# Splitting the 512-column matmul of a compensated projection into 256-column matmuls that alternate between the halves of a PSUM bank

## The chip, the cores and the metric

The kernel runs on one core of a Trainium2 chip. The metric is the device time of one execution in microseconds (us): the median of three runs before the change is 1472.32 us (1472.12 to 1472.53). A number in ns is marked so.

## The reference

The kernel computes one layer of a hybrid decoder trunk on a sequence of 256 tokens with 2048 features, in float32. What matters here are its projections:

```python
h = rms_norm(x, norm_mix_g[l])
proj = h @ w_in[l]                      # 2048 x 10240
...                                      # HGRN2, S5 and stick-breaking mixers on proj, a GLU (512 x 1024)
merged = sum_k sigmoid(gate_k) * (branch_k @ w_branch[k])   # 3 x (512 x 2048), shortened
x = x + merged @ w_out[l]               # 2048 x 2048
hf2 = rms_norm(x, norm_ffn_g[l])
up = causal_depthwise_conv(hf2 @ w_up[l], conv_w[l])        # 2048 x 11264
x = x + (jax.nn.silu(up[..., :D_FF]) * up[..., D_FF:]) @ w_down[l]   # 5632 x 2048
```

## The kernel before

**Tiles and blocks.** Everything is transposed: a tile of a projection is 128 output features (partitions) by 256 tokens (columns), and it is a sum over blocks. A block is one 128x128 piece of a weight matrix times 128 input features by 256 tokens. The projections that go through the function `piece` have 3680 blocks: 80 tiles of 16 blocks for w_in (1280), 8 tiles of 4 for the GLU (32), 16 tiles of 16 for w_out (256), 88 tiles of 16 for w_up (1408) and 16 tiles of 44 for w_down (704).

**Three passes.** To keep float32 accuracy with the type fp32r, each weight and each input is split in a high and a low part, and a block is three products: high weight times high input, high weight times low input, low weight times high input. Inputs lie in SBUF as `[P, k, 2, SEQ]`, the high part's 256 columns ahead of the low part's 256. So one matmul of 512 columns (L295) with the high weight writes the whole PSUM bank: columns 0 to 255 hold the sum with the high input, 256 to 511 that with the low input. A second matmul of 256 columns (L297) adds the low weight's product to columns 0 to 255. When a tile is complete, ScalarE copies the upper half of the bank to SBUF (`copy_half`, L577) and VectorE adds the lower half to it (`add_halves`, L846). There are four such banks, used in turn.

**The branches** go through another function, `branch_piece` (L309): its three passes are three matmuls of 256 columns, all into columns 0 to 255 of the bank; 192 blocks in all.

**The ring of weights.** Weights come in pieces of up to 8 blocks (512 KB). The DMA queue of SyncE loads a piece into one of four `raw` buffers (L245), ScalarE rounds it to `w_hi` (L570), VectorE subtracts to get `w_lo` (L841), TensorE multiplies and increments `piece_used`. ScalarE waits for `piece_used` before it overwrites a `w_hi`, VectorE waits for ScalarE, TensorE waits for `lo_ready`, and SyncE waits for `lo_ready` before it reloads a `raw`.

**Order of the work.** Every engine has its program written out by hand. During the w_in projection (tiles n = 0 to 79) the work of the three mixers is woven in between tiles: the tables AT and TABLE_AT (L95 to L101) say after which tile each engine does which part. TensorE's mixer products are plain float32 matmuls (`fp32_product`, L328), VectorE's and GpSimd's mixer steps stand in the same in-order programs as the weights' `w_lo`. Behind w_in come the GLU, the branches, w_out, w_up and w_down, in loops.

Of the kernel before, what the change touches and what calls it, by code (L numbers as in the profile page):

```python
# [45 lines left out]
P = 128  # L46
D_MODEL = 2048
SEQ = 256
# [66 lines left out]
def layer(nc, xT, w_in, w_glu, w_br, w_out, w_up, w_down, norm_mix, norm_ffn, hg_gain, s5_small, s5_b, s5_c,  # L115
          s5_skip, sb_gain, conv, out):
    ctx = ExitStack()
    with ctx:
# [75 lines left out]
        bank = [ctx.enter_context(nc.psum_tensor(f"bank{b}", [P, 512], F32)) for b in range(BANKS)]  # L194
# [92 lines left out]
        def _(pe):  # L287
            def piece(b, p, c, blocks, rhs, first, last):

                if p is not None:  # L290
                    pe.wait_ge(lo_ready, p + 1)
                w, l = w_hi[c % RING], w_lo[c % RING]
                for n, k in enumerate(blocks):
                    a = rhs(n)
                    pe.matmul(bank[b][:, :], w[:, k * P:(k + 1) * P], a.rearrange("p a t -> p (a t)"),  # L295
                              start=first and n == 0, stop=False, skip_group_check=True)
                    mm = pe.matmul(bank[b][:, 0:SEQ], l[:, k * P:(k + 1) * P], a[:, 0, :],  # L297
                                   start=False, stop=last and n == len(blocks) - 1, skip_group_check=True)
                return mm

            def branch_piece(b, p, c, lo, src):
# [145 lines left out]
            def a_in_block(n, k):  # L447
                if n == 0:
                    pe.wait_ge(S("a_in_lo"), k + 1)
                return a_in[:, k, :, :]  # L450

            for n in range(IN_TILES):
                bank_free(n)
                for h in range(2):
                    mm = piece(n % BANKS, 2 * n + h, 2 * n + h, range(PIECE), lambda k: a_in_block(n, PIECE * h + k), h == 0, h == 1)
                    mm.then_inc(piece_used, 1)
                mixers(n)
# [3 lines left out]
            for m in range(CT):  # L461
                for i in range(2):
                    n = GLU_T + 2 * m + i
                    bank_free(n)
                    mm = piece(n % BANKS, GLU_P + m if i == 0 else None, GLU_P + m, range(CT * i, CT * (i + 1)),
                               lambda k: glu_in[:, k, :, :], True, True)
                    mm.then_inc(piece_used if i else S("glu_first"), 1)
# [19 lines left out]
            def after(sem, j, k, src):  # L487

                if j == 0:
                    pe.wait_ge(S(sem), k + 1)  # L490
                return src[:, k, :, :]

            with pe.Fori(0, OUT_TILES // BANKS) as i:
                for j in range(BANKS):
                    bank_free(i * BANKS + (OUT_T + j))
                    for h in range(2):
                        mm = piece(j, i * (2 * BANKS) + (OUT_P + 2 * j + h), 2 * j + h, range(PIECE),
                                   lambda k: after("merged_lo", j, PIECE * h + k, a_in), h == 0, h == 1)
                        mm.then_inc(piece_used, 1)
# [17 lines left out]
            with pe.Fori(0, DOWN_TILES // BANKS) as i:  # L517
                c = 0
                for j in range(BANKS):
                    bank_free(i * BANKS + (DOWN_T + j))  # L520
                    at = 0
                    for blocks in DOWN_PIECES:
                        if j == 0:
                            pe.wait_ge(S("act_lo"), at + blocks)
                        mm = piece(j, i * (BANKS * len(DOWN_PIECES)) + (DOWN_P + c), c, range(blocks),
                                   lambda k: act[:, at + k, :, :], at == 0, at + blocks == FT)
# [947 lines left out]
```

## Time and profile before

| what | value |
|---|---|
| median of 3 runs | 1472.32 us |
| the profiled execution's own time | 1471.41 us |
| its span (first to last instruction) | 1469.7 us |
| TensorE busy with matmuls | 1414.2 us, 96% of the span |
| VectorE busy | 1079.3 us, 73% |
| ScalarE busy | 761.9 us, 52% |
| GpSimd busy | 380.2 us, 26% |
| mean granted TensorE clock | 0.988 of 2.4 GHz |

Times are those of one execution under the profiler. PE is TensorE's matmul side, PEld its weight loads (which run beside matmuls), DVE is VectorE, ACT is ScalarE, POOL is GpSimd. The duration that a matmul's row shows goes from its start to its last result, and consecutive matmuls overlap; the distance between two starts is what a matmul takes in a stream.

### The profile page before, as it was taken

What the parts mean: (1) busy time and instruction counts of PE and PEld (TensorE: products, weight loads), DVE (VectorE), ACT (ScalarE), POOL (GpSimd) and SP (SyncE); (2) the same over time, 40 slices, a digit from 0 to 9 for tenths busy, and PEclk for the clock granted to TensorE, in tenths of its full rate; (3) what the DMA queues carried; (4) which work ended last, traced back from release to release, by engine and by line L of the source; (5) the groups of instructions that cost most, each with busy time, mean ns of one, the idle gap of its engine ahead of it and who ended that gap; (6) DMA issues with size and microseconds to landing.
All of it is one profiled execution on the core that took longest, in us unless ns stands there. A gap on an engine that the chain in (4) does not pass through costs nothing.

```text
span 1469.7 us, 24906 instructions
## 1 busy us (share of the span) xinstructions
PE 1414.2 (96%) x8320; PEld 1248.5 (85%) x8320; DVE 1079.3 (73%) x1370; ACT 761.9 (52%) x1050; POOL 380.2 (26%) x337
## 2 busy tenths in 40 slices
PE   5999999998888989999999999999999999999999
PEld 4889888887666878998888888888888888888887
DVE  5897757879999957777668777777777776544543
ACT  5564456675344445444565555555555554444432
POOL 5044312254966631332211111111111110000000
PEclk9999999999998999999999999999999999999999
DMA  7555544453434455565556555656555555666663
GB/s 216 175 175 170 166 151 161 150 182 108 144 128 151 151 165 195 200 214 186 187 173 205 194 183 188 197 181 194 191 181 197 187 186 187 182 213 202 189 202 111
DMA packets 74338, 261.45 MB, mean 178 GB/s; under 512 B 8560, under 2 KB 9104, under 8 KB 74160
## 3 DMA queue, kind: packets, MB, share of 16 engines
q1 hardware_dynamic: 73152, 256.41, 54.0%
q0 software_dynamic: 992, 4.37, 0.8%
q8 instruction: 31, 0.51, 0.1%
q14 instruction: 19, 0.16, 0.0%
q10 hardware_dynamic: 144, 0.01, 0.0%
HBM read 258.66 MB, written 2.10 MB: 177 GB/s over the span
## 4 chain that ended last, share of the span: by engine, by line
PE 76%; DVE 14%; issue 4%; POOL 2%; ACT 2%; DMA 1%; SPq 0%; POOLq 0%; ACTq 0%; DVEq 0%
PE bank L295 48%; PE bank L297 25%; DVE w_lo L841 5%; DVE tmp L849 3%; PE pair L328 2%; DVE tmp L1092 2%; DVE tmp L856 1%; DMA gates<-xT 1%; PE bank L309 1%; ACT w_hi L570 1%; POOL proj L1280 1%; POOL merged L1371 1%; POOL merged L1373 1%; DVE gates L846 0%; DVE proj L846 0%
## 5 line engine op out<-in xcount | busy, mean ns | idle before, releaser
L841 DVE TENSOR_TENSOR w_lo<-raw,w_hi 128x1024 fp32r<-128x1024 f32 x500 | 632.1, 1274 | 321.0 <-ACT w_hi L570 317.2
L570 ACT ACTIVATE w_hi<-raw 128x1024 fp32r<-128x1024 f32 x500 | 512.1, 1030 | 438.7 <-PE bank L297 380.1
L295 PE MATMUL bank<-a_in,w_hi 128*128 128x512 f32 x1536 | 553.9, 401 | 42.7 <-DVE w_lo L841 40.8
L295 PE MATMUL bank<-h,w_hi 128*128 128x512 f32 x1408 | 488.4, 390 | 0.0
L297 PE MATMUL bank<-a_in,w_lo 128*128 128x256 f32 x1536 | 438.8, 286 | 0.0
L297 PE MATMUL bank<-h,w_lo 128*128 128x256 f32 x1408 | 397.1, 282 | 0.0
L295 PEld LDWEIGHTS bank<-a_in,w_hi 128*128 128x128 f32 x1536 | 295.2, 192 | 114.6 <-issue 35.5
L295 PEld LDWEIGHTS bank<-h,w_hi 128*128 128x128 f32 x1408 | 264.2, 188 | 55.4
L297 PEld LDWEIGHTS bank<-a_in,w_lo 128*128 128x128 f32 x1536 | 297.2, 194 | 0.5 <-issue 0.5
L297 PEld LDWEIGHTS bank<-h,w_lo 128*128 128x128 f32 x1408 | 266.1, 189 | 0.0
L295 PE MATMUL bank<-act,w_hi 128*128 128x512 f32 x704 | 244.1, 390 | 0.0
L297 PE MATMUL bank<-act,w_lo 128*128 128x256 f32 x704 | 198.5, 282 | 0.0
L1398 POOL TENSOR_TENSOR padded<-sum_u,rstd 128x256 f32<-128x256 f32 x88 | 73.8, 839 | 413.2 <-DVE sum_u L846 400.4
L295 PEld LDWEIGHTS bank<-act,w_hi 128*128 128x128 f32 x704 | 132.1, 188 | 27.7
L297 PEld LDWEIGHTS bank<-act,w_lo 128*128 128x128 f32 x704 | 133.1, 189 | 0.0
L1311 POOL TENSOR_TENSOR gates<-gates,rstd 128x256 f32<-128x256 f32 x48 | 57.8, 1210 | 155.9 <-DVE gates L846 155.1
L577 ACT ACTIVATE half<-bank 128x256 f32<-128x256 f32 x208 | 75.6, 366 | 9.0 <-PE bank L297 9.0
L1311 POOL TENSOR_TENSOR proj<-proj,rstd 128x256 f32<-128x256 f32 x32 | 32.9, 1038 | 135.6 <-DVE proj L846 99.1
L782 ACT ACTIVATE silu<-convd 128x256 f32<-128x256 f32 x43 | 18.0, 418 | 96.0 <-DVE convd L1214 96.0
L1212 DVE SCALAR_TENSOR_TENSOR convd<-padded,taps,convd 128x256 f32<-128x256 f32 x88 | 62.8, 713 | 1.0 <-ACT convd L802 1.0
L1214 DVE SCALAR_TENSOR_TENSOR convd<-padded,taps,convd 128x256 f32<-128x256 f32 x88 | 53.9, 613 | 11.5
L1280 POOL TENSOR_TENSOR proj<-tmp 128x512 f32<-128x512 f32 x32 | 56.3, 1760 | 1.9
(165 smaller groups left out, 1083.3 us busy)
## 6 DMA issues: line engine op xcount, KB each, us to landing
raw<-w_up SPq DMA_DIRECT2D x176, 512.0 KB, 3.3
raw<-w_in SPq DMA_DIRECT2D x160, 512.0 KB, 4.0
raw<-w_down SPq DMA_DIRECT2D x80, 512.0 KB, 4.3
raw<-w_out SPq DMA_DIRECT2D x32, 512.0 KB, 3.8
raw<-w_br SPq DMA_DIRECT2D x16, 512.0 KB, 3.6
raw<-w_br SPq DMA_DIRECT2D x16, 256.0 KB, 3.4
raw<-w_down SPq DMA_DIRECT2D x16, 256.0 KB, 2.7
gates<-xT SPq DMA_DIRECT2D x4, 512.0 KB, 10.4
```

Of the source, the lines that this page charges most:

```text
L295: pe.matmul(bank[b][:, :], w[:, k * P:(k + 1) * P], a.rearrange("p a t -> p (a t)"), start=first and n == 0, stop=False, skip_group_check= ...
L297: mm = pe.matmul(bank[b][:, 0:SEQ], l[:, k * P:(k + 1) * P], a[:, 0, :], start=False, stop=last and n == len(blocks) - 1, skip_group_check ...
L328: mm = pe.matmul(out_[p0:p1, c0:c1], lhsT, rhs, start=start, stop=stop, skip_group_check=True)
L570: act_e.activation(w_hi[s][:, 0:blocks * P], raw[s][:, 0:blocks * P], ACT.Copy).then_inc(hi_ready, 1)
L577: act_e.activation(half[j % 2][:, :], bank[j % BANKS][:, SEQ:2 * SEQ], ACT.Copy).then_inc(half_copied, 1)
L841: ve.tensor_tensor(w_lo[s][:, w], raw[s][:, w], w_hi[s][:, w].bitcast(F32), ALU.subtract).then_inc(lo_ready, 1)
L849: link(ve, ve.tensor_tensor(out_, a, b, op), name)
L1212: ve.scalar_tensor_tensor(c, padded[:, j % 2, 1:SEQ + 1], taps[:, t, 1:2], c, ALU.mult, ALU.add).then_inc(S("tap1"), 1)
L1214: ve.scalar_tensor_tensor(c, padded[:, j % 2, 0:SEQ], taps[:, t, 0:1], c, ALU.mult, ALU.add).then_inc(S("conv_done"), 1)
L1280: link(pool, pool.tensor_tensor(out_, a, b, op), name)
L1311: pool.tensor_tensor(proj(n), proj(n), rstd[:, :], ALU.mult).then_inc(tile_scaled, 1)
L1398: pool.tensor_tensor(padded[:, j, 2:], sum_u[:, j, :], rstd[:, :], ALU.mult).then_inc(S("up_scaled"), 1)
```

## The change

In `piece`, the 512-column matmul and the 256-column matmul of a block become three matmuls of 256 columns. For an even block of a piece they go to the lower, upper and lower half of the bank: high weight with high input, high weight with low input, low weight with high input. For an odd block the first two are exchanged, and the halves are upper, lower, upper: high weight with low input, high weight with high input, low weight with high input. So consecutive matmuls never write the same half. What a half holds differs from before, the sum of the two halves doesn't. Only the first matmul of a tile has the start flag. `branch_piece`, the mixers' products and all other engines stay as they are.

```diff
                 for n, k in enumerate(blocks):
                     a = rhs(n)
-                    pe.matmul(bank[b][:, :], w[:, k * P:(k + 1) * P], a.rearrange("p a t -> p (a t)"),
-                              start=first and n == 0, stop=False, skip_group_check=True)
-                    mm = pe.matmul(bank[b][:, 0:SEQ], l[:, k * P:(k + 1) * P], a[:, 0, :],
-                                   start=False, stop=last and n == len(blocks) - 1, skip_group_check=True)
+                    cols = slice(k * P, (k + 1) * P)
+                    passes = ((w, 0), (w, 1), (l, 0)) if n % 2 == 0 else ((w, 1), (w, 0), (l, 0))
+                    for m, (x, part) in enumerate(passes):
+                        at = (n + m) % 2 * SEQ
+                        mm = pe.matmul(bank[b][:, at:at + SEQ], x[:, cols], a[:, part, :], start=first and n == 0 and m == 0,
+                                       stop=last and n == len(blocks) - 1 and m == 2, skip_group_check=True)
                 return mm
```

## Rows read from the trace of the kernel before

**Rows 1.** Busy time by stretch of the span, in us (x instructions).
```profile
core 0: us, PE busy (x) PEld busy (x) DVE busy (x) ACT busy (x) POOL busy (x), PEclk, DMA share, GB/s
57.00:340.00 283.00, 281.29 (x1670) 248.30 (x1670) 221.72 (x246) 168.75 (x199) 95.44 (x68) 1.00 0.50 164
340.00:524.00 184.00, 153.21 (x858) 126.89 (x858) 169.34 (x167) 79.30 (x92) 131.03 (x79) 0.93 0.44 143
649.00:1470.00 821.00, 816.42 (x4708) 723.52 (x4708) 560.86 (x737) 418.61 (x618) 96.79 (x123) 1.00 0.58 187
```

**Rows 2.** Waits of TensorE from 340 to 524 us: total, times, longest.
```profile
PE bank L295 <- DVE w_lo L841: 24.6, 10, 4.9
PE pair L328 <- POOL proj L1280: 6.2, 2, 4.4
```

**Rows 3.** Waits of TensorE from 524 us to the end.
```profile
PE bank L309 <- DVE o_s L1136: 1.5, 1, 1.5
PE bank L295 <- DVE a_in L1151: 0.8, 1, 0.8
```

**Rows 4.** Other engines' waits, 340 to 524 us.
```profile
ACT w_hi L570 <- PE bank L297: 63.3, 32, 5.9
DVE w_lo L841 <- ACT w_hi L570: 8.5, 10, 1.5
DVE proj L1097 <- PE pair L328: 2.8, 1, 2.8
```

**Rows 5.** Line L295: duration ns min/median/max, first and last start in us.
```profile
L295 PE MATMUL bank<-h,w_hi x1408: 390/390/588, 733.3 to 1221.5; 128*128 128x512 f32 x176
L295 PE MATMUL bank<-act,w_hi x704: 390/390/390, 1221.9 to 1465.6; 128*128 128x512 f32 x176
```

**Rows 6.** TensorE in order of time, w_up: start us, us.
```profile
899.80 0.39 PE L295 MATMUL bank<-h,w_hi 128*128 128x512 f32 x1
900.03 0.28 PE L297 MATMUL bank<-h,w_lo 128*128 128x256 f32 x1
900.15 0.39 PE L295 MATMUL bank<-h,w_hi 128*128 128x512 f32 x1
```

**Rows 7.** Line L309 from 580 to 643.65 us, columns as in rows 5.
```profile
L309 PE MATMUL bank<-o_hg,w_hi x120: 277/279/281, 580.5 to 640.5; 128*128 128x256 f32 x120
```

**Rows 8.** TensorE in order of time, branches: a block's first two matmuls a row.
```profile
587.53 0.39 PE L309 MATMUL bank<-o_s,w_hi 128*128 128x256 f32 x2
...
587.88 0.40 PE L309 MATMUL bank<-o_s,w_hi 128*128 128x256 f32 x2
...
588.58 0.40 PE L309 MATMUL bank<-o_s,w_hi 128*128 128x256 f32 x2
...
588.93 0.39 PE L309 MATMUL bank<-o_hg,w_hi 128*128 128x256 f32 x2
...
589.28 0.40 PE L309 MATMUL bank<-o_hg,w_hi 128*128 128x256 f32 x2
```

**Rows 9.** TensorE in order of time: plain float32 products of a mixer.
```profile
288.11 0.59 PE L328 MATMUL pair<-tmp,lower 128*128 128x256 f32 x2
288.54 0.38 PE L328 MATMUL pair<-tmp,ones 128*128 128x128 f32 x2
288.76 0.60 PE L328 MATMUL pair<-tmp,lower 128*128 128x256 f32 x2
```

**Rows 10.** TensorE in order of time, at a granted clock of 0.5.
```profile
33.08 0.63 PE L295 MATMUL bank<-a_in,w_hi 128*128 128x512 f32 x1
33.51 0.41 PE L297 MATMUL bank<-a_in,w_lo 128*128 128x256 f32 x1
33.72 0.63 PE L295 MATMUL bank<-a_in,w_hi 128*128 128x512 f32 x1
```

**Rows 11.** Weight loads by line, form and tile: count, busy us, mean ns.
```profile
L297 PEld LDWEIGHTS bank<-a_in,w_lo 128*128 128x128 f32 x1536 | 297.2, 194 | 0.5 <-issue 0.5
L309 PEld LDWEIGHTS bank<-o_hg,w_hi 128*128 128x128 f32 x128 | 19.5, 188 | 0.0
```

## The prediction

> **What bounds the kernel now.** I read the busy time by stretch first, then the waits of TensorE in each stretch, then the distances between its starts. From 57 to 340 us and from 649 us to the end TensorE is busy for 281.29 of 283 us and 816.42 of 821 us, at full clock [rows 1]. From 524 us on it waits twice, for 2.3 us together [rows 3]. So there every nanosecond added to a block moves the end. From 340 to 524 us it is otherwise: TensorE has 153.21 busy us of 184, VectorE 169.34 [rows 1]; TensorE waits 24.6 us for VectorE's w_lo and 6.2 us for GpSimd [rows 2], while VectorE waits 11.3 us for anybody and ScalarE 63.3 us for TensorE's pieces [rows 4]. VectorE's mixer work sets the pace there, and a somewhat slower TensorE finds its cover in its own waits.
>
> **The price of a block before.** In w_down the 704 blocks start their wide matmul from 1221.9 to 1465.6 us: 243.7 / 703 = 346.66 ns a block [rows 5]. w_up gives (1221.5 - 733.3) / 1407 = 347.0 with a norm's product inside. The starts show the parts: after the 512-column start the next comes 0.23 us later, after the 256-column start 0.12 us later [rows 6]. At 2.4 GHz the 768 columns alone are 320 ns; 26.7 ns are lost on two matmuls.
>
> **The price after.** The change removes 3680 matmuls of 512 columns and their weight loads and adds twice as many of 256 columns, each with a weight load of its own: three loads a block where there were two. The columns stay 768. The trace shows this very stream, except for the alternation: the branches. Blocks start there at 587.53, 587.88, 588.58, 588.93 and 589.28 us: five blocks in 1.75 us, 350 ns each [rows 8]. Over a longer stretch, the 120 matmuls of the o_hg tiles run from 580.5 to 640.5 us [rows 7]. First to last are 14 groups of 36 matmuls (three tiles of 12) and 10 more, 514 steps: 60.0 / 514 = 116.7 ns each, 350.2 a block. I take 350.1, so a block costs 3.4 ns more (0.1 us of rounding in each of the two starts is 0.6 ns a block, so 2.8 to 4.0). The third load has room: a load's row is 188 ns long in the branches and 194 in w_in [rows 11], and the branches' pace is reached with three of them, so their overlap with matmuls is in the 350.
>
> The alternation has no row. Two rows bound it. In float32 products a group of 256 columns takes 0.43 us in two records [rows 9], which is the time of four sweeps of 256 columns at full clock (0.427), and the 128 columns behind it add to columns just written, at 0.22 us for two records. Sums into the same columns one straight behind the other run at full pace there, so same-half repetition isn't what costs 10 ns a matmul in the branches, and avoiding it should give nothing. The bank changes at 588.93 us, and the step into it is 350 ns like the others [rows 8], so a change of address costs nothing visible either. I take zero. The ends: below, the float32 pace, 0.43 / 4 = 107.5 ns a matmul, 322.5 a block, 24.2 ns less than before; above, the step behind the narrow matmul as it stands now between wide ones, 0.12 us (900.03 to 900.15, rounded) [rows 6], 360 a block, 13.3 ns more than before.
>
> **Which blocks count.** From 524 us to the end there are 112 of w_in's blocks, 32 of the GLU, 256, 1408 and 704, which is 2512: times 3.4 ns = 8.5 us. From 57 to 340 us 704 blocks: 2.4 us. VectorE is tied to TensorE through the ring in that stretch, so the delay is handed on. From 340 to 524 us 368 blocks, 1.25 us, against 30.8 us of waits: I count 0.3. The first 96 blocks wait for x and the first weights; those at half clock cost nothing, since there a block is 0.64 us (33.08 to 33.72), exactly 768 columns at 1.2 GHz [rows 10], and three times 256 columns are the same: 0. Sum 11.2 us. Nothing else is issued differently: no DMA, no wait, no increment is added, pieces are released in the same places; ScalarE's and VectorE's copies of the halves come after the last matmul of the tile as before. VectorE with 560.86 us of 821 [rows 1] isn't near the path.
>
> 1471.4 + 11.2 = 1482.6 us for the profiled execution; it stood 0.9 us below the median, so the median becomes 1483.5. I say 1483.
>
> The Trainium skill (TensorE: Matmul & The Clock Gate, "Back-to-back issue gap") puts a warm matmul's gap at N / 2.4 plus 2.5 ns. By it a block would go from 325 to 327.5 ns and the change would cost 2.5 ns a block, 8.3 us in all over the 3312 blocks, an estimate. The trace differs on the level (346.7 and 350), and nearly agrees on the step.
>
> **Rivals.**
> 1. *Alternation gives time back.* If the 27 ns that a block loses come from adding to columns still in flight, three matmuls that take turns go at 107.5 ns: 3312 uncovered or handed-on blocks (all but the first stretch's 96, less 272 of the middle one) times -24.2 ns = -80 us, 1392 us; half of the effect gives 1432. For it: the loss per matmul is there [rows 6, 8] and has no cause in the rows. Against it: the float32 sums [rows 9], and that the wide matmul, whose second half follows on other columns, loses more than a narrow one (0.23 us less 0.213 = 0.017, against 0.010 in the branches). Chance 0.15.
> 2. *The jump between halves isn't free.* TensorE pays on each of the three steps when the next matmul starts in the other half, up to the 0.12 us that it takes behind the narrow one [rows 6]: 13.3 ns a block times 3312 = 44 us, 1516 us; half of the way from the branches' pace (355 ns) gives 1499. For it: there is a jump from one half to the whole bank in every block, and the two matmuls lose 26.7 ns where two of the branches lose 20 [rows 6, 7]. Against it: the jumps between banks [rows 8]. Chance 0.13, more of it at 1499 than at 1516. It is dearer than the forecast from the point where a step is above 118 ns.
> 3. *It doesn't show.* The alternation gives back just the 3.4 ns, or the added time is covered where I think it isn't: within 3 us of 1472.3. Little speaks for it, since there is 2.3 us of wait behind 524 us. Chance 0.07.
>
> **How the numbers follow.** The forecast has 0.65. Its own range is 1479 to 1487: 2.8 to 4.0 ns over 3312 blocks is 9.3 to 13.2 us, and the middle stretch can move some 2 us either way, since its waits end in short spells at half clock that shift. For 8 in 10 the range reaches down to the edge of rival 3 and up over most of rival 2: 1471 to 1503. Left out are rival 1 and the dear end of rival 2, some 0.19. What a measurement of this kernel can tell from no change is about 0.2%, 3 us. Faster has rival 1 (0.15), same rival 3 (0.07), slower the forecast and rival 2 (0.78).
>
> **What would show it.** Right: narrow matmuls of w_down start 116.7 ns apart, 350 ns a block, w_down's blocks last 246.1 us instead of 243.7, w_up's and w_out's grow in the same ratio of 1.01; the weight loads number 12,000 where 8320 were; the stretch that was 340 to 524 us is as long as before; branches unchanged. Wrong: a step of 107 to 113 ns (rival 1), of 118 or more (rival 2), or steps that depend on which half comes next.

## The result and the profile after

The changed kernel takes 1485.35 us in the median of six runs, against 1472.42 us before; the ratio is 1.0089 (95% interval 1.0074 to 1.0104): slower by 0.9%, which is clear of the noise. (The ratios here and below are estimated from all runs, so they can differ a little from the quotient of the two medians.) The six runs are not one cloud: 1481.1, 1481.8 and 1482.0 us, and 1488.7, 1489.4 and 1489.5 us. The granted clock doesn't tell the groups apart, 0.988 to 0.991 in the lower and 0.988 in the upper. The profiled execution is of the upper group: its own time is 1489.53 us, its span 1487.9. No run of the lower group was profiled.

The page's busy times, with their instruction counts:

```profile
PE 1434.8 (96%) x12000; PEld 1419.6 (95%) x12000; DVE 1080.0 (73%) x1370; ACT 762.8 (51%) x1050; POOL 379.8 (26%) x337
```

The count is the forecast one: 3680 more matmuls and loads. VectorE, ScalarE and GpSimd do what they did. By stretch (columns as in [rows 1], whose first two stretches these answer to; the third is all that lies behind; the bounds were set by hand, so the lengths of the stretches don't measure the delay):

```profile
57.00:342.40 285.40, 284.06 (x2378) 279.50 (x2379) 222.60 (x247) 169.68 (x200) 95.57 (x68) 1.00 0.50 163
342.40:526.00 183.60, 154.49 (x1229) 145.79 (x1228) 168.98 (x166) 78.59 (x92) 130.50 (x79) 0.93 0.44 144
524.40:1488.00 963.60, 957.42 (x8118) 956.48 (x8114) 650.74 (x880) 484.52 (x714) 132.34 (x164) 1.00 0.59 184
```

TensorE's waits in the middle stretch [rows 2] and behind it [rows 3] are now:

```profile
PE bank L299 <- DVE w_lo L843: 21.8, 9, 4.8
PE pair L330 <- POOL proj L1282: 7.4, 3, 4.4
```

```profile
PE bank L311 <- DVE o_s L1138: 1.5, 1, 1.5
PE bank L299 <- DVE a_in L1153: 0.6, 1, 0.6
PE bank L311 <- DVE gated L1162: 0.5, 1, 0.5
```

Now the pace, which is the time from one block's start to the next block's. The rows of the narrow low-weight matmul, one a block, answer to [rows 5]; the first is w_out seen through a window, then w_up and w_down of the whole run:

```profile
L299 PE MATMUL bank<-a_in,w_lo x234: 277/279/280, 656.0 to 737.5; 128*128 128x256 f32 x117
...
L299 PE MATMUL bank<-h,w_lo x1408: 277/278/280, 737.9 to 1235.4; 128*128 128x256 f32 x176
...
L299 PE MATMUL bank<-act,w_lo x704: 278/278/278, 1235.7 to 1484.1; 128*128 128x256 f32 x176
```

Divide each by its count less one. w_out: 81.5 / 233 = 349.8 ns a block, the forecast pace. w_down: 248.4 / 703 = 353.3 ns, and w_up 353.6 with the norm's product inside. The same code runs at two paces in one execution; below, 350 ns is called the quick pace and 353.3 the slow one. The starts in w_down, two matmuls in the first row of each pair:

```profile
1300.15 0.40 PE L299 MATMUL bank<-act,w_hi 128*128 128x256 f32 x2
1300.39 0.28 PE L299 MATMUL bank<-act,w_lo 128*128 128x256 f32 x1
1300.51 0.40 PE L299 MATMUL bank<-act,w_hi 128*128 128x256 f32 x2
1300.74 0.28 PE L299 MATMUL bank<-act,w_lo 128*128 128x256 f32 x1
1300.86 0.40 PE L299 MATMUL bank<-act,w_hi 128*128 128x256 f32 x2
```

The slow pace begins behind the norm's float32 product, which TensorE does after w_up's first tile. Ahead of it 15 blocks take 5.25 us (737.85 to 743.10), 350 ns each; behind it 1391 steps take 491.5 us, 353.3 ns each:

```profile
737.85 0.28 PE L299 MATMUL bank<-h,w_lo 128*128 128x256 f32 x1
...
743.10 0.28 PE L299 MATMUL bank<-h,w_lo 128*128 128x256 f32 x1
743.22 0.59 PE L330 MATMUL pair<-root,ones 128*128 128x256 f32 x2
```

```profile
L299 PE MATMUL bank<-h,w_lo x1392: 278/278/278, 743.9 to 1235.4; 128*128 128x256 f32 x199
```

The branches show both paces too, and their code is the same in every run. Here are the low-weight matmuls of one of the three branches: from 583 to 640 us in the trace of before, from 583 to 640 us in that of experiment 11, whose code is that of before until w_up begins at 733 us, and from 597 to 650 us in that of the changed kernel:

```profile
L309 PE MATMUL bank<-o_s,w_lo x56: 277/279/281, 583.6 to 639.2; 128*128 128x256 f32 x56
...
L314 PE MATMUL bank<-o_s,w_lo x56: 281/281/281, 582.9 to 639.1; 128*128 128x256 f32 x56
...
L311 PE MATMUL bank<-o_s,w_lo x48: 280/280/280, 599.3 to 647.0; 128*128 128x256 f32 x48
```

A tile of this branch has 4 blocks, and 8 blocks of the others lie between two such tiles. So 14 tiles are 159 steps, and 12 tiles are 135. That makes 55.6 / 159 = 349.7 ns, 56.2 / 159 = 353.5 and 47.7 / 135 = 353.3.

### The profile page after: what moved, and what is told of

Same layout as the page of the kernel before. It is cut to its first block, busy times and chain, and to the rows that moved or that the text cites. A ratio compares the mean times of both kernels' runs of the same rounds, so it can differ in the third digit from the quotient of the medians.

```text
span 1487.9 us, 32266 instructions
## 1 busy us (share of the span) xinstructions
PE 1434.8 (96%) x12000; PEld 1419.6 (95%) x12000; DVE 1080.0 (73%) x1370; ACT 762.8 (51%) x1050; POOL 379.8 (26%) x337
## 4 chain that ended last, share of the span: by engine, by line
PE 75%; DVE 15%; issue 4%; POOL 2%; DMA 2%; ACT 2%; SPq 0%; POOLq 0%; DVEq 0%; ACTq 0%
PE bank L299 72%; DVE w_lo L843 5%; DVE tmp L851 3%; PE pair L330 2%; DVE tmp L1094 2%; DMA raw<-w_in 1%; DVE tmp L858 1%; ACT w_hi L572 1%; POOL proj L1282 1%; POOL merged L1373 1%; DMA raw<-w_br 1%; POOL merged L1375 1%; DVE gates L848 0%; DVE tmp L1087 0%; DVE proj L848 0%
## 5 line engine op out<-in xcount | busy, mean ns | idle before, releaser
L299 PE MATMUL bank<-a_in,w_hi 128*128 128x256 f32 x3072 | 559.9, 285 | 39.3 <-DVE w_lo L843 37.7
L299 PEld LDWEIGHTS bank<-a_in,w_hi 128*128 128x128 f32 x3072 | 479.9, 193 | 47.9 <-issue 31.4
L299 PE MATMUL bank<-h,w_hi 128*128 128x256 f32 x2816 | 497.7, 281 | 0.0
L299 PEld LDWEIGHTS bank<-h,w_hi 128*128 128x128 f32 x2816 | 427.9, 188 | 0.1
L299 PE MATMUL bank<-h,w_lo 128*128 128x256 f32 x1408 | 391.4, 278 | 0.0
L299 PE MATMUL bank<-act,w_hi 128*128 128x256 f32 x1408 | 248.8, 280 | 0.0
L299 PEld LDWEIGHTS bank<-act,w_hi 128*128 128x128 f32 x1408 | 213.9, 188 | 0.0
L1282 POOL TENSOR_TENSOR proj<-tmp 128x512 f32<-128x512 f32 x32 | 56.2, 1756 | 1.9
```

The lines of the kernel that those rows point to most:

```text
L299: mm = pe.matmul(bank[b][:, at:at + SEQ], x[:, cols], a[:, part, :], start=first and n == 0 and m == 0, stop=last and n == len(blocks) - 1 ...
L1282: link(pool, pool.tensor_tensor(out_, a, b, op), name)
```

## The experiments

Paces are read as above. w_up's count includes one norm product, some 0.3 ns a block. The diffs are shortened; from experiment 6 on the lines of w_up and w_down, which a flag of `piece` chooses between, stand below each other.

**1. No alternation.**

```diff
-                    passes = ((w, 0), (w, 1), (l, 0)) if n % 2 == 0 else ((w, 1), (w, 0), (l, 0))
+                    passes = ((w, 0), (w, 1), (l, 0))
                     for m, (x, part) in enumerate(passes):
-                        at = (n + m) % 2 * SEQ
+                        at = SEQ if first and n == 0 and m == 1 else 0
```

> Three 256-column matmuls a block as in the changed kernel, but all in the lower half of the bank (only a tile's first high-weight times low-input pass goes to the upper half), as the branches do it. Theory (the cost is that of three matmuls in place of two, the alternation does nothing, and the stream has two steady paces, 350.0 and 353.3 ns a block, which it takes on at a restart): blocks at 350.0 or 353.3 ns and no other, times between 1481 and 1490 us, some runs near 1481.5 and some near 1489. Rival A (the alternation causes the 353.3): 350.0 throughout, all runs at 1481 to 1483. Rival B (the alternation saves something that sums into the same half cost): slower than the changed kernel, 1492 us or more.

Measured: 1481.34 us, ratio 1.0078 (1.0062 to 1.0095). Single runs: 1480.8, 1480.8, 1481.2, 1481.5, and 1486.4, 1488.2. The profiled one is of the first kind:

```profile
L299 PE MATMUL bank<-h,w_lo x1408: 277/279/281, 736.0 to 1228.9; 128*128 128x256 f32 x176
...
L299 PE MATMUL bank<-act,w_lo x704: 274/279/281, 1229.3 to 1475.3; 128*128 128x256 f32 x176
```

246.0 / 703 = 349.9 ns. Without alternation the times are those of the changed kernel, with a lower and an upper group again. So the alternation neither costs nor saves anything that these runs can tell, and sums into one half straight behind each other cost no more than alternating ones, as [rows 9] had suggested. No run of the upper group was profiled here, so its pace wasn't read.

**2 and 3. One projection alone.** `piece` gets a flag, and only w_down's call (2) or only w_in's call (3) splits.

```diff
-                                   lambda k: act[:, at + k, :, :], at == 0, at + blocks == FT)
+                                   lambda k: act[:, at + k, :, :], at == 0, at + blocks == FT, split=True)
```

> The change in w_down alone (704 blocks), all else as before. Theory: +3.3 ns a block at the one pace is 2.3 us, +6.7 ns at the other is 4.7 us, so 1474.8 or 1477.1 us, with one pace through nearly all of w_down in a run. Rival (the slower pace grows out of the long unbroken stream before it, not out of the restart): always 4.7 us.

> The change in the w_in projection alone (1280 blocks, of which 368 lie between 340 and 524 us). Theory (what is added before 340 us is handed on, what is added from 340 to 524 us is covered by TensorE's waits for VectorE): 816 uncovered blocks times 3.3 to 4 ns is 2.7 to 3.3 us, 1475.1 to 1475.7 us, and TensorE's waits in the middle stretch get shorter. Rival (VectorE's mixer work sets the pace up to 524 us whatever TensorE does before it): at most 112 blocks count, 0.4 us, 1472.8 us.

Measured for w_down: 1473.78 us against 1472.03, ratio 1.0009 (1.0000 to 1.0018), 1.8 us. All eleven runs lie between 1472.35 and 1474.68 us, below the 1477.1 us of the slow pace. The profiled run's pace is the quick one, (1469.0 - 1222.9) / 703 = 350.1 ns:

```profile
L305 PE MATMUL bank<-act,w_lo x704: 277/279/280, 1222.9 to 1469.0; 128*128 128x256 f32 x176
```

Measured for w_in: 1472.70 us, ratio 1.0002 (0.9993 to 1.0011), +0.7 us and inside the noise: the rival's figure, not the 2.7 to 3.3 us of my theory. TensorE's waits from 340 to 524 us are hardly shorter than in [rows 2], 29.7 us in place of 30.8:

```profile
PE bank L305 <- DVE w_lo L849: 22.3, 10, 4.8
PE pair L336 <- POOL proj L1288: 7.4, 3, 4.3
```

What became of the delay is seen in VectorE's program. The same instruction is read at three places, first before, then in the fully changed kernel:

```profile
105.92 2.52 DVE L841 TENSOR_TENSOR w_lo<-raw,w_hi 128x1024 fp32r<-128x1024 f32 x1
339.29 2.36 DVE L841 TENSOR_TENSOR w_lo<-raw,w_hi 128x1024 fp32r<-128x1024 f32 x2
504.89 2.36 DVE L841 TENSOR_TENSOR w_lo<-raw,w_hi 128x1024 fp32r<-128x1024 f32 x2
```

```profile
105.93 2.53 DVE L843 TENSOR_TENSOR w_lo<-raw,w_hi 128x1024 fp32r<-128x1024 f32 x1
340.49 2.36 DVE L843 TENSOR_TENSOR w_lo<-raw,w_hi 128x1024 fp32r<-128x1024 f32 x2
505.39 2.36 DVE L843 TENSOR_TENSOR w_lo<-raw,w_hi 128x1024 fp32r<-128x1024 f32 x2
```

The changed kernel is not late at 106 us, 1.2 us late at 340 and 0.5 us late at 505. So half of the 2.4 us forecast for the first stretch arrives at 340 us, and the middle stretch gives 0.7 us back. The growth of 1.2 us from 106 to 339 us stands in the traces of experiments 1, 3, 4 and 5 as well; of it 0.4 to 0.9 us are left at 505 us in these four.

**4. A restart ahead of every four tiles.**

```diff
+            def restart():
+                pe.matmul(pair[(M["norm2"] + 1) % 2][:, 0:P], ones[:, :], eye[:, :], start=True, stop=True, skip_group_check=True)
+
+            wait_taken(pe, "s5_y3")
             with pe.Fori(1, UP_TILES // BANKS) as i:
+                restart()
                 up_body(i)
...
             with pe.Fori(0, DOWN_TILES // BANKS) as i:
+                restart()
```

> The changed kernel with one small float32 product (128 columns, result not used) ahead of every four tiles in w_up and w_down, 25 in all. Theory (each product or wait is a restart at which the stream takes on one of two paces): stretches of 350.0 and 353.3 ns a block alternate between the products, so the single runs lie closer together than the 1481.1 to 1489.5 us of the changed kernel, around 1485 plus some 4 us for the products (25 times 0.16). Rival (the pace belongs to the run or to the stage): one pace from product to product, and times in two groups 7 us apart, near 1485 and 1493.

Measured: 1487.66 us, ratio 1.0106 (1.0092 to 1.0121), runs from 1487.1 to 1488.4, one group. But the two paces don't alternate: w_down's row is 246.8 / 703 = 351.1 ns, which is 350.0 with three products of 0.25 us in between, and a window between two products gives 14.0 / 40 = 350 ns:

```profile
L299 PE MATMUL bank<-act,w_lo x704: 274/279/281, 1235.5 to 1482.3; 128*128 128x256 f32 x176
...
L299 PE MATMUL bank<-h,w_lo x41: 277/280/281, 785.8 to 799.8; 128*128 128x256 f32 x41
```

The coin toss is wrong: behind this product the pace is the quick one in all 25 places of this trace. It was the quick one ahead of the first product too, behind the norm's, so this trace has no place where a product turned the pace. The products cost more than thought, (1487.66 - 1481.34) / 25 = 0.25 us each against the median of experiment 1.

**5. One restart.** The same product once, behind `up_body(0)` (w_up's first four tiles), ahead of the loop. The semaphore wait that stands ahead of it, `wait_taken(pe, "s5_y3")`, doesn't hold TensorE up in the trace.

> The changed kernel with a single small float32 product (128 columns, result not used) on TensorE behind the first four tiles of w_up, the last restart before 2000 blocks without one. Theory (the pace is taken on at a restart, and behind such a product it is the quick one, as behind all 25 of the run before): every run at 1481 to 1482 us plus 0.25 us, none near 1489, and 350.0 ns a block from about 760 us to the end. Rival (the low spread of the run before was chance, or the pace belongs to the run): two groups near 1481.5 and 1489.

Measured: 1481.30 us, ratio 1.0062 (1.0049 to 1.0076), five runs from 1480.95 to 1481.88 us, none near 1489. The profiled run shows both paces, ahead of the product and behind it:

```profile
L299 PE MATMUL bank<-h,w_lo x46: 278/278/279, 742.0 to 757.9; 128*128 128x256 f32 x46
```

```profile
L299 PE MATMUL bank<-h,w_lo x1342: 277/279/282, 759.9 to 1229.3; 128*128 128x256 f32 x192
```

15.9 / 45 = 353.3 ns, then 469.4 / 1341 = 350.0. One product of 0.25 us turned the pace in this execution, and no run is in the upper group. If each run fell into either group like a tossed coin, five in the lower one would come about once in 32; the four runs of experiment 4 form one group too.

**6. Narrow weight loads.** Of all but a tile's first block only 64 weight columns are loaded and used.

```diff
+                    wide = not (first and n == 0)
+                    few = slice(k * P, k * P + (P // 2 if wide else P))
+                    passes = ((w, few, 0, 256), (w, few, 256, 512), (l, few, 0, 256))    # w_up
+                    passes = ((w, few, 0, 512), (l, few, 0, 256))                        # w_down
```

> Weight loads of 64 columns in place of 128 for all but a tile's first block: in w_up with three 256-column matmuls a block (no alternation), in w_down with 512 and 256 as before. Output features 64 to 127 of these tiles are left out of the sums but for the first block. Theory A (each matmul start costs its 10 to 15 ns whatever is loaded): 350 or 353 ns a block in w_up, 346.7 in w_down, 1477 to 1481 us. Theory B (the weight load, nearly as long as a 256-column matmul, holds the next matmul up): both paces fall towards the bare 320 ns, w_up by 1400 times 20 ns and more, under 1450 us.

```profile
L316 PE MATMUL bank<-h,w_lo x1408: 277/280/284, 733.1 to 1232.7; 128*128 128x256 f32 x88, 128*64 128x256 f32 x88
...
L316 PE MATMUL bank<-act,w_lo x704: 276/280/283, 1233.1 to 1476.8; 128*64 128x256 f32 x160, 128*128 128x256 f32 x16
```

Measured in one run: 1482.33 us; w_up 499.6 / 1407 = 355.1 ns, w_down 243.7 / 703 = 346.7. The narrow loads' own rows are shorter, some 134 ns where a load of 128 columns has 188:

```profile
L316 PEld LDWEIGHTS bank<-act,w_hi x704: 133/134/188, 1232.7 to 1476.4; 128*64 128x64 f32 x160, 128*128 128x128 f32 x16
```

They buy nothing in the pace, so theory B falls. w_up is even 1.8 ns above the slower of the two paces, which stays unexplained.

**7. Other lengths.**

```diff
+                        passes = ((w, cols, 0, 512), (l, cols, 0, 512))                             # w_up
+                        passes = ((w, cols, 0, 384), (w, cols, 384, 512), (l, cols, 0, 256))        # w_down
```

> w_up: the low weight's matmul takes 512 columns too (it adds the low weight times low input product), two equal matmuls a block; w_down: three unequal matmuls of 384, 128 and 256 columns. Theory (a fixed cost a matmul plus a cost by column): w_up 2 x 228.3 = 457 ns a block, w_down 350 to 353 ns as with three equal ones. Rival (a load needs about 107 ns to be hidden, so a 128-column matmul can't hide the next load): w_down at 350 plus about 50, near 400 ns.

```profile
L316 PE MATMUL bank<-h,w_lo x1408: 389/397/399, 733.9 to 1390.9; 128*128 128x512 f32 x176
...
L316 PE MATMUL bank<-act,w_lo x704: 330/332/336, 1391.4 to 1675.7; 128*128 128x256 f32 x176
```

Measured in one run: 1681.32 us. w_up: 657.0 / 1407 = 467.0 ns, 233.3 for each 512 columns, where 457 was expected: as much as two matmuls of 256 in the branches (2 x 116.7). w_down: 284.3 / 703 = 404.4 ns, the rival's figure, though the run doesn't show that the load is what the 128 columns fail to hide. The starts in w_down, the matmuls of 384 and 128 columns in one row:

```profile
1500.19 0.33 PE L316 MATMUL bank<-act,w_lo 128*128 128x256 f32 x1
1500.36 0.40 PE L316 MATMUL bank<-act,w_hi 128*128 128x384 f32 x2
1500.59 0.33 PE L316 MATMUL bank<-act,w_lo 128*128 128x256 f32 x1
```

The step from the 256-column matmul to the next is 0.17 us in place of 0.12, so the 50 ns are lost one matmul behind the short one.

**8. A narrow low load beside a wide matmul, and six matmuls of 128 columns.**

```diff
+                        passes = ((w, cols, 0, 512), (l, few, 0, 256))                              # w_up
+                        passes = (tuple((w, cols, i * P, (i + 1) * P) for i in range(4))            # w_down
+                                  + tuple((l, cols, i * P, (i + 1) * P) for i in range(2)))
```

> w_up: 512 and 256 columns as before, but the low weight's load has 64 columns (low product left out for output features 64 to 127 but in the first block); w_down: six matmuls of 128 columns a block. Theory: w_up at 346.7 ns still if a load costs nothing by its width, less by up to 13 ns if the step behind the wide matmul is the low weight's load; w_down 6 x 63 = 380 ns if only a fixed 10 ns a matmul counts, 6 x 109 = 654 ns if a load sets the floor of a step (the float32 products of 128 columns start 109 to 112 ns apart).

Measured in one run: 2022.84 us. w_up is at its old pace, (1221.6 - 733.4) / 1407 = 347.0 ns. For w_down two windows (first two rows) and the busy times of two stretches (columns as in [rows 1]):

```profile
L316 PE MATMUL bank<-act,w_hi x653: 272/274/278, 1224.8 to 1334.0; 128*128 128x128 f32 x164
...
L316 PE MATMUL bank<-act,w_lo x326: 272/274/278, 1225.0 to 1333.7; 128*128 128x128 f32 x163
```

```profile
1222.00:1334.00 112.00, 112.00 (x1006) 112.00 (x1005) 33.40 (x39) 25.78 (x32) 0.84 (x1) 1.00 0.35 102
1346.00:1782.00 436.00, 436.00 (x2045) 436.00 (x2046) 57.43 (x60) 47.26 (x53) 0.53 (x1) 0.50 0.18 53
```

109.2 us for 978 steps is 111.7 ns a matmul of 128 columns, hardly less than one of 256 takes. By 1346 us the granted clock has fallen to half, and it stays there. Between the two stretches TensorE stood still once, with nothing awaited that the profile shows:

```profile
1341.64 0.94 PE L316 MATMUL bank<-act,w_hi 128*128 128x128 f32 x4 [1.68 <-issue]
```

**9. bf16.** The upper two bytes of each number, stride 2, are read as bf16: three matmuls a block in w_up, two in w_down.

```diff
+                def top(x):
+                    return x.bitcast(BF).rearrange("p (n two) -> p n two", two=2)[:, :, 1]
```

> All operands of w_up and w_down are read as bf16 (the upper two bytes of each fp32r number, stride 2): w_up with three 256-column matmuls a block, w_down with 512 and 256. The results of these two projections are left at bf16 accuracy. Theory (TensorE's 9% over the bare 320 ns belongs to streams of fp32r): w_up and w_down both come to 320 to 328 ns a block, about 1430 us. Rival (it belongs to any stream of separate matmuls with their own loads): 350 to 353 and 346.7 ns as with fp32r, 1477 to 1481 us.

```profile
L304 PE MATMUL bank<-h,w_lo x1408: 273/276/278, 733.8 to 1219.6; 128*128 128x256 bf16 x176
...
L304 PE MATMUL bank<-act,w_lo x704: 273/273/273, 1219.9 to 1459.0; 128*128 128x256 bf16 x176
```

Measured in one run: 1464.49 us, w_up 345.3 ns, w_down 239.1 / 703 = 340.1. Neither theory: most of the loss over 320 ns is there in bf16 too, and the third matmul costs 5 ns a block there.

**10. The order of the lengths.**

```diff
+                if mode == "pairs":          # w_up: wide, wide, narrow, narrow
+                    todo = [todo[i + j] for i in range(0, len(todo), 4) for j in (0, 2, 3, 1)]
+                if mode == "grouped":        # w_down: all wide ones of a piece, then all narrow ones
+                    todo = todo[0::2] + todo[1::2]
```

> 512 and 256 columns as before the change, in another order: in w_up two blocks at a time, wide, wide, narrow, narrow; in w_down all wide matmuls of a piece, then all narrow ones. Theory (equal neighbours run at 116.7 ns per 256 columns whatever their length, and 346.7 is what a change of length from one matmul to the next gives): about 348 ns in w_up, 350 in w_down, 1475 to 1477 us. Rival (two matmuls a block instead of three are what makes 346.7): 346.7 in both, 1472 us.

```profile
L320 PE MATMUL bank<-h,w_lo x1408: 280/281/282, 734.2 to 1222.2; 128*128 128x256 f32 x176
L320 PE MATMUL bank<-act,w_hi x704: 389/394/398, 1222.3 to 1468.0; 128*128 128x512 f32 x176
L320 PE MATMUL bank<-act,w_lo x704: 277/279/281, 1224.2 to 1468.6; 128*128 128x256 f32 x176
```

Measured in one run: 1474.18 us. w_down lasts from 1222.3 us to the start of its last matmul at 1468.6 plus 0.1: 246.4 / 704 = 350.0 ns with two matmuls a block, as theory said. w_up keeps about 346.8 ((1222.2 - 734.2) / 1407), as the rival said.

**11. Some blocks split.**

```diff
+                    if every and n % every == every - 1:        # every = 2 in w_up, 4 in w_down
+                        for part in range(2):
+                            pe.matmul(bank[b][:, part * SEQ:(part + 1) * SEQ], w[:, k * P:(k + 1) * P], a[:, part, :],
```

> The kernel before with only some blocks' wide matmul split in two of 256 columns: every second block in w_up (2.5 matmuls a block), every fourth in w_down (2.25). Theory A (trains of equal length go at 116.7 ns per 256 columns, trains in which lengths change within a few matmuls at 115.6, whatever the count): 346.7 ns a block in both stages, 1471 to 1472 us. Theory B (each matmul beyond two adds 3.3 ns): 348.3 in w_up and 347.5 in w_down, 1408 x 1.7 + 704 x 0.8 = 2.9 us, 1474.3 us.

```profile
L302 PE MATMUL bank<-h,w_lo x1408: 277/280/282, 733.4 to 1227.1; 128*128 128x256 f32 x176
L302 PE MATMUL bank<-act,w_lo x704: 277/280/282, 1227.4 to 1473.5; 128*128 128x256 f32 x176
```

Measured in one run: 1479.03 us; w_up 350.9 ns, w_down 246.1 / 703 = 350.1. Both theories fall: one block in four split already costs all blocks what splitting every block costs.

## Why the prediction was right, and where it wasn't

The sign and the mechanism hold: the split stream goes at a pace of its own, and behind 524 us nothing covers it. The median is 12.9 us above before where 11.2 was forecast; the middle of the lower group is 9.4 us above it, that of the upper group 17.0.

**The price of a block**, 350.1 ns from the branches' rows [rows 7, 8], was right for the quick pace: 349.8 in w_out, and 349.9 and 350.1 ns in w_down in experiments 1 and 2. It was too low for the upper group. The step that failed is that one stretch of the branches was taken for the only pace of the stream. In the profiled execution w_up and w_down go at 353.3. Their 2112 blocks then cost 6.7 ns each instead of 3.3, 14.1 us against 7.0; these 7.0 us are nearly all of the 7.6 between the groups' middles, 1489.4 and 1481.8. The trace of before had one pace in the branches and no hint of another. The sign "branches unchanged" failed with it: in the changed kernel's trace they run at 353.3 ns from 597 us on, which is some 0.5 us of the 18.1 us between the two profiled executions. Experiment 5's trace shows that a product on TensorE can turn the pace behind w_up's first tile. That the two groups of runs are the two paces fits the sums and the nine runs of experiments 4 and 5, but only one run of the upper group was profiled.

**The alternation at zero** was right (experiment 1). Rival 1 (time given back) is gone; so is rival 2 (a jump between halves that costs), though its 118 ns a step came up: 353.3 / 3 = 117.8. It doesn't need a jump between halves: the branches, which never jump within a tile, run at 353.3 ns in the changed kernel and in experiment 11, and in experiment 5's trace the same alternating code runs at either pace.

**Which blocks count** was right behind 524 us and wrong ahead of it. I had handed on 2.4 us from the first stretch, on the ground that VectorE is tied to TensorE through the ring; half of that arrives at 340 us. At 505 us VectorE's program is 0.5 us late, and the change in w_in alone costs 0.7 us, which the measurement can't tell from nothing. VectorE's mixer work sets the pace in the middle stretch, and the slack in TensorE's waits there (30.8 us) can cover a late start as well as slower blocks. Why nothing is added up to 106 us is open. With that the lower group adds up: 2512 x 3.3 ns = 8.3 us, and 0.3 from w_in's blocks ahead of 524 us (the 0.7 less 112 x 3.3 ns, which the 2512 hold already), make 8.6 us, 1481.0 us; measured 1481.1 to 1482.0.

So there were two errors of opposite sign: some 2 us too much from the first stretches, and a second pace that adds 7 us in half of the runs. That the median lies near the forecast is luck. It is the middle of a gap between 1482.0 and 1488.7 us in which no run lies, because the six runs fell three and three; four against two would have given about 1482 or 1489. The own range of the likeliest case, 1479 to 1487 us, missed three of the six single runs.

**What the 26.7 ns are** I had put down to the two matmuls of a block. That reading isn't borne out: two matmuls of 512 columns lose 20 ns each over the 213.3 of their columns (experiment 7), in a train of equal ones a 512 costs what two 256s cost, and two matmuls a block run at 350.0 when their lengths are grouped (experiment 10). Strictly wide-narrow, or two and two, gives 346.7; trains of equal lengths, or a mixture with a split block now and then, give about 350. Why is open. What the runs show is that the change costs time because it leaves the pattern that runs at 346.7, which has the same number of columns. Three matmuls and three loads a block aren't needed for that, since 350.0 comes with two of each (experiment 10); the width of the loads (experiment 6) and the place of the sums (experiment 1) have no part in it either.

## What to carry to other kernels

Where the same stream of matmuls runs elsewhere in the kernel, its distance between starts is a good price for a rewrite (350.1 ns against 349.8 to 350.1 here); but read it from several stretches, because one stream can have more than one steady pace and keep it for 2000 blocks. Splitting a matmul into equal parts of the same columns cost 1 to 2% of a block here and can't be made up by where the sums go. Time added ahead of a stretch that another engine sets can be given back in that stretch: count it at its end, not at its start.

## What the runs showed of the hardware

- A stream of 256-column matmuls, each with its own weight load, has steady paces of 116.7 and 117.8 ns, in code that the change doesn't touch too (the branches in experiment 11). In fp32r the pattern of 512 and 256 columns in turn had the one pace of 346.7 in w_up and w_down of every trace that has it. A float32 product of 128 columns put between two tiles was followed by the first of them in all 25 places of experiment 4 and in experiment 5. Behind the norm's product of 256 columns either pace followed: 353.3 ns in the changed kernel, 350.1 in experiment 4. What picks the pace is open.
- A matmul of 128 columns in fp32r takes 111.7 ns in a stream, 5 ns less than one of 256. At half clock its steps are 436 us / 2045 = 213 ns, and there one of 256 columns takes as long (0.21 us, [rows 10]).
- In that stream of 128-column matmuls the granted clock was 1.00 (2.4 GHz) for the first 112 us, fell to 0.50 (1.2 GHz) where TensorE had stood still for 1.68 us, and stayed there, although TensorE then shows as busy for all 436 of 436 us. Why it didn't rise again is open; the streams of 256 and 512 columns kept 1.00.
